# Moving the prompt's expert selection from ahead of the convolution into the query and key loop

## The reference, cut to what matters

```python
def peer_ffn(h, w_query, sub_keys, u_tab, v_tab):        # expert layer
    s = einsum('thpk,hpnk->thpn', qry, sub_keys)         # 8 heads x 2 x 128 scores
    s1, i1 = top_k(s[:, :, 0], 16); s2, i2 = top_k(s[:, :, 1], 16)
    cand = s1[..., :, None] + s2[..., None, :]           # 16 x 16 sums
    sc, ci = top_k(cand, 16)
    e = take(i1, ci // 16) * 128 + take(i2, ci % 16)
    g = softmax(sc)
    act = gelu(einsum('thkd,td->thk', u_tab[e], hc))
    return einsum('thk,thkd->td', g * act, v_tab[e])

def mixer(h, lp, l, ctx):                                # latent tokens
    z = h @ w_in
    u = a * sigmoid(b); y = depthwise_conv31(u) + conv_b; y = silu(layer_norm(y))
    q, k = rms_norm(q), rms_norm(k)                      # per head of 64, four of them: dq, dk, nq, nk
    q, k = axial_rope(q), axial_rope(k)                  # dq and dk only
    ...
```

## Time and profile before

| | us |
|---|---|
| median of 3 executions | 5191.51 |
| lowest and highest | 5183.64 and 5203.18 |
| the profiled execution | 5183.64 |
| its span in the trace | 5181.8 |
| PE busy | 4446.4 (86%) |
| DVE busy | 3367.6 (65%) |
| ACT busy | 1876.2 (36%) |
| POOL busy | 1768.5 (34%) |

### The profile page before, as it was taken

How to read it: one execution, slowest core, us unless ns; L and a number is a source line. 1 busy time by engine, 2 the same in 40 slices (tenths; PEclk the granted TensorE clock), 3 DMA queues, 4 the chain that set the end, 5 groups by cost and what they waited for, 6 DMA issues and landing times.

```text
span 5181.8 us, 46814 instructions
## 1 busy us (share of the span) xinstructions
PE 4446.4 (86%) x14388; PEld 2296.5 (44%) x14388; DVE 3367.6 (65%) x7266; ACT 1876.2 (36%) x5016; POOL 1768.5 (34%) x1600
## 2 busy tenths in 40 slices
PE   7889998987799888888888998998779987777777
PEld 4674464334545333344544445633454632222222
DVE  4238656777787677675444876777778767676544
ACT  1210243443233434565533014543323343333333
POOL 3007202323243453443332460223224443344332
PEclk9899989998899999999999998999889999999999
DMA  8752227998799999999999130499879999999998
GB/s 290 255 180 75 90 101 270 347 343 342 311 420 419 414 420 420 412 397 418 406 420 403 57 114 17 162 346 347 337 284 420 418 413 422 421 421 420 421 421 351
DMA packets 277114, 1677.26 MB, mean 324 GB/s; under 512 B 31808, under 2 KB 31856, under 8 KB 112384
## 3 DMA queue, kind: packets, MB, share of 16 engines
q0 software_dynamic: 190896, 1365.43, 65.1%
q1 hardware_dynamic: 82944, 302.03, 16.0%
q10 hardware_dynamic: 3024, 6.82, 0.3%
HBM read 1667.33 MB, written 6.82 MB: 323 GB/s over the span
## 4 chain that ended last, share of the span: by engine, by line
PE 39%; DMA 39%; DVE 10%; ACT 7%; issue 5%; POOL 0%; SPq 0%; DVEq 0%; ACTq 0%; POOLq 0%
DMA arena<-experts,bsb 25%; PE ps L2196 13%; DMA arena<-experts,peidx 11%; PE ps L1783 8%; PE ps L1958 6%; DVE arena L1686 3%; PE ps L1891 2%; DMA wring<-w 2%; DVE arena L1384 2%; PE ps L2048 2%; PE ps L2070 2%; ACT L1047 1%; PE ps L1759 1%; ACT T L1051 1%; PE ps L2107 1%
## 5 line engine op out<-in xcount | busy, mean ns | idle before, releaser
L2196 PE MATMUL ps<-arena,T 128*128 128x512 f32 x4096 | 1966.1, 613 | 443.2 <-ACT T L1051 442.2
L1686 DVE CUSTOM_DVE_ANT_0 arena<-arena,h_sb 128x1024 f32<-128x1024 f32 x1024 | 1252.6, 1227 | 866.1 <-DMA arena<-experts,bsb 861.3
L665 POOL DMA_INDIRECT arena<-experts,bsb x1024 | 1093.3, 1068 | 1723.8 <-PE ps L2196 1590.3
L2196 PEld LDWEIGHTS ps<-arena,T 128*128 128x128 f32 x4096 | 725.5, 191 | 1567.1 <-ACT T L1051 941.0
L1047 ACT ACTIVATE bsb<-T 128x1 f32<-128x1 f32 x1024 | 205.9, 201 | 1316.6 <-DVE T L1686 1314.9
L1783 PE MATMUL ps<-h_sb,wring 128*128 128x256 f32 (+2 forms) x2304 | 527.0, 386 | 35.2 <-DVE h_sb L1424 13.7
L2107 PE MATMUL ps<-h_sb,wring 128*128 128x512 f32 x1024 | 478.3, 622 | 61.3 <-DVE arena L1611 58.0
L648 POOL DMA_INDIRECT arena<-experts,peidx x256 | 287.6, 1124 | 703.6 <-DVE arena L1384 648.3
L1783 PEld LDWEIGHTS ps<-h_sb,wring 128*128 128x128 f32 x2304 | 386.6, 198 | 187.5 <-issue 151.9
L1051 ACT ACTIVATE T<-ident,bsb 128x128 f32<-128x128 f32 x1024 | 410.9, 401 | 33.6
L1374 DVE CUSTOM_DVE_ANT_0 arena<-arena,h_sb 128x1024 f32<-128x1024 f32 x256 | 312.8, 1222 | 155.0 <-DMA arena<-experts,peidx 153.7
(11 more groups left out here) (319 smaller groups left out, 4415.4 us busy)
## 6 DMA issues: line engine op xcount, KB each, us to landing
wring<-w SPq DMA_DIRECT2D x576, 512.0 KB
arena<-experts,bsb POOLq DMA_INDIRECT x1024
bsb<-bias POOLq DMA_DIRECT2D x16, 512.0 KB, 3.8
arena<-subk POOLq DMA_DIRECT2D x4, 1024.0 KB, 7.3
arena<-v_scratch POOLq DMA_DIRECT2D x64, 64.0 KB, 2.0
arena<-experts,peidx POOLq DMA_INDIRECT x256
x_sb<-xT POOLq DMA_DIRECT2D x1, 2048.0 KB, 14.2
v_scratch<-arena ACTq DMA_DIRECT2D x8, 256.0 KB, 2.0
```

Of the source, the lines that this page charges most:

```text
L665: gp.indirect_dma_start(rows[:, n % NS, :], None, experts, bass.IndirectOffsetOnAxis(ap=eidx[:, t % 2, i:i + 1], axis=0)).then_inc(row_in[ ...
L1686: v.tensor_tensor_reduce(e, e, htok(t), 1.0, 0.0, ALU.mult, ALU.add, dots[:, t % 2, i:i + 1]).then_inc(dot, 1)
L2196: mm = pe.matmul(ps[:, 6 + half, :], diag[:, n % ND, :], rows[:, n % NS, D + half * 512:D + (half + 1) * 512], start=(i == 0), stop=(i == ...
```

## The change

The generator is made later, behind the convolution. No step stands ahead of the multiplies of L1463 any more, and each iteration of the loop from 1 on does up to 9 steps in place of 2.

```diff
                 v.wait_ge(u_zero, l + 1)
-                routing_steps = prompt_route(l)
                 for c in range(4):
-                    for _ in range(28):
-                        next(routing_steps)
                     wait_unit(v, u(f"ca{c}"))
                     wait_freed(v, u(f"cb{c}"))
                     v.tensor_tensor(U[:, c, PAD:PAD + LAT], ...)
...
+                routing_steps = prompt_route(l)
                 for n in range(NQ + 1):
                     if n < NQ:
                         qk_mean(n)
                     if n >= 1:
                         qk_norm(n - 1)
-                        for _ in range(2):
+                        for _ in range(9):
                             next(routing_steps, None)
```

## The result

After the change the kernel takes 5218.02 us (median of 7 runs, 5212.19 to 5227.35), against 5184.69 us before (7 runs, 5171.51 to 5203.18) on the same chip. The ratio is 1.0063, with a 95% interval of 1.0043 to 1.0084: slower by 33 us. The median of before was 5191.51 over the three executions that the forecast started from, and is 6.8 us lower over seven. The profiled execution took 5220.28 us, its span is 5218.5 us, 36.7 us more than that of before. The forecast was 5225 us within 5206 to 5244, and slower.

A forecast was written before the change was run, and what follows sets the result against it. PE was taken to bound the projections and the query and key loop. Removal gives 0; per layer 14.8 us of loop delay plus 1.8 of clock make 16.6, for two 33, so 5191.51 becomes 5225 us, within 5206 to 5244.

The forecast's parts named there:

- What is removed: Ahead of the convolution multiplies: taking the 112 steps away gains 0, since PE never waits there.
- The rival that DVE held up the projections: Projections: an earlier convolution gives up to 3.14 us a layer, 5218 us total; its chance is inside the forecast's 0.73.
- T(6): PE's transposes number 6 in the query and key loop: a new wait for DVE of some 3.5 us.
- T(8): PE's transposes number 8 in the loop: a wait of some 3.3 us, and 9.2 us late.
- wide steps: Six selection steps on DVE, 1.26 us each, falling in loop iteration 8, whose steps take 8.4 us.
- The wait for ACT at iteration 7: Before loop iteration 7: DVE's existing 2.8 us wait, until ACT has squared the convolution and unit 7, is kept.
- T(15): PE's last transposes in the loop: a wait of about 6 us; layer 14.8 us late, 16.6 with the clock's 1.8.
- The slower unit behind T(8): PE's 16 matmuls after that wait run at a lowered clock: 1.8 us more, passed on once a layer.
- The slower unit behind T(6): PE's matmuls after that wait: a lowered clock there is harmless, since DVE is the later one until iteration 9.
- The clock did not stay down: Denies a rival: half rate from T(6) to the loop's end, some 45 us a layer, about 5315 us total; chance 0.04.
- The 5.4 us of iteration 16: Steps behind the last normalising: free, hidden in DVE's wait before the first score reduction, with 4 us left.
- The absorbing loop: Rival for the query and key loop: spare time takes the steps, only 10.6 us left, 5202 us; chance 0.20.

The follow-up runs named there:

- second experiment: The kernel before with all 140 selection steps ahead of the four convolution multiplies and none in the loop: 5207.09 us, ratio 1.0049.
- second profile: The changed kernel run and profiled once more, nothing altered, against the kernel before: 5216.65 us against 5180.35, ratio 1.0078.
- the placed version: The changed kernel with each iteration's number of steps fitted to its room, none in iteration 15 and 29 behind the last normalising: 5202.48 us, ratio 1.0026.

## Why the prediction was right

**What is removed.** Taken as 0, with PE busy throughout. It is: the fourth multiply came at 414.07 for 414.05. The rival that DVE held up the projections fell with it, and so did its 3.14 us. (This is for taking steps away. That adding 28 there is not free was seen in the second experiment.)

**The walk through the loop.** T(6) was to wait 3.5 us and waited 4.21. T(8) was to wait 3.3 and waited 2.70. Iteration 8 was to be 13.15 long (4.75 + 8.4, wide steps included) and was 13.05. T(8) was to be 9.2 us late and was: 591.53 - 2.07 - 580.25 = 9.2. The wait for ACT at iteration 7 was kept at 2.79. T(10) to T(13) have no wait. T(14) and T(15) were to wait 3.5 and 6 and waited 3.65 and 5.88. One piece was wrong: T(7) was to wait 1 us and did not. The unit before it took 8.04 instead of 7.03, and DVE's L1513 for T(7) ended at 580.82: with a unit of 7.03 the wait would have been about half a us, and the clock's price behind T(6) filled its place.

**The clock.** The slower unit behind T(8) was taken at 1.8 us more and had 8.73 - 7.03 = 1.70. The slower unit behind T(6) came (8.04) and was free, as told. That the price falls behind T(8) was in part luck: in layer 1 of the second profile it fell behind T(6), and the layer was 3.5 us shorter. The clock did not stay down: in the loop it was 0.97.

**The end of a layer.** T(15) was to be 14.8 + 1.8 = 16.6 us late. It is 644.49 - 2.07 - 625.84 = 16.6, where 625.84 is its start before; in layer 1 it is 17.5. The 5.4 us of iteration 16 were to be hidden with 4 us left, and DVE waits 4.15. That cover is thin. Longer tails use it up: the four runs with more steps there paid.

**The sum.** Two layers at 16.6 were 33 us, and the medians differ by 33.3. (That 5218.02 lies 7 us under the forecast of 5225 is the 6.8 us by which the first median of before was high.) Some of that agreement is luck. The profiled spans differ by 36.7: 2.1 before the first projections, 16.8 in the loop of layer 0, 2.4 from there to the projections of layer 1, 18.0 from there to its first score reduction (0.6 of them ahead of the loop), and -2.5 after it. Inside the 2.4 the attention of layer 0 gives back: its last score matmul is only 11.2 us late, not 18.9, and the merge and the experts take that again. The attention's start has its clock at 0.77 where it was 0.62. In layer 1, where the clock was the lower one, nothing is given back: the last score matmul is as late as the first reduction, within 1 us. I had said that this stretch may move by 5 us a layer, and had counted nothing for it.

**The rivals.** The absorbing loop was to decide at a delay of T(8) of under 5 us; it was 9.2. It is not far off as an idea: placed by iteration, the same steps let T(15) come 0.8 us late. What defeats the even 9 is made in three places. T(7) is 6.3 us late, by the steps of iterations 2 to 6, the wait for ACT and the slower unit. T(9) is 11.0 us late, by the six wide steps that one iteration gets, and the unit behind T(8). T(15) is 16.6 us late, by the nine steps between the last two normalisings. Taking either of the last two places alone away gave back 5.5 and 4.4 us at the first score reduction (17.1 less 11.6, and less 12.75), after the longer tails had taken more than 1 us again. The first place was not taken away alone, but the run without steps in iteration 8 shows it by itself, as 6.6 us from T(7) to T(14), and the placed version without it.

## What to carry to other kernels

Fillers between the steps of a pipelined loop are paid by the iteration in which they fall, not by their sum: write down for each iteration what room it has, and look for the longest filler, for waits that an iteration already has, and for the last iterations, where nothing follows that could take up the delay. The largest delay can hide another one, which then shows when the largest is taken away. Idle time of an engine that waits for the bound engine is the free place for fillers, as long as nothing else is shifted there: a shift of 9.6 us turned a meeting of two engines in which only POOL, which had time, was held up into one that cost DVE 12.9 us. A wait of the same few us in every variant, such as the 3.46 at T(14), is worth more attention than the fillers around it.

## What the runs showed of the hardware

A copy on POOL that begins 5 us after a row of 120 two-input DVE instructions lasted 75.14 us, until they were done; alone it takes 0.61. Where POOL had begun its means before the row, its work went on (27.78 us busy of the first 31.5), and the same DVE row took 92.46 us instead of 79.59. Who pays turned on a shift of 9.6 us. That the order in which they meet decides it is suggested by this but not shown: in the second case a further copy of POOL, begun 0.8 us after the row, was not shut out (1.07 us). The Trainium skill, in "GPSIMD Engine Reference", section "8. Key points", says that POOL shares its SBUF interfaces with VectorE and contends with its instructions that have two SBUF inputs. By that rule the two hinder each other here; the traces agree, and add by how much.

The unit of 16 matmuls, 7.03 us in an unbroken row, took 8.73 behind a wait of 2.70 us, 9.11 behind one of 10.29, and behind one of 4.21 once 8.04 and once 9.38. Behind a wait of 1.59 it took 7.03. The granted clock was 0.57 in the 3.5 us behind T(6) in the changed kernel's profile, 0.65 behind T(8), and 0.50 where the unit took 9.38. So the price of a wait does not simply grow with its length, and equal waits had different prices.
